# First-index one-hots made on GpSimd per token, and eight expert blocks beside the gate spreading in three rounded products

## The reference

```python
q = (hf @ wq).reshape(T, PEER_HEADS, 2, PEER_DQ // 2)
s = jnp.einsum('thcd,hckd->thck', q, subkeys).astype(jnp.float32)
v_top, i_top = lax.top_k(s, PEER_TOPK)
...
ids = jnp.take_along_axis(cand_i, best_pos, axis=-1)
g = jax.nn.softmax(best_s, axis=-1)
...
act = jax.nn.gelu(jnp.einsum('tkd,td->tk', ub, xb).astype(jnp.float32))
return jnp.einsum('tk,tkd->td', (gb * act).astype(xb.dtype), vb)
```

## Time and profile before

| | |
|---|---|
| time, median of 3 runs | 2134.61 us (2133.51 to 2137.69) |
| profiled execution, its own time | 2135.38 us |
| its span, first to last instruction | 2133.6 us |
| mean granted TensorE clock | 0.988 of full speed |
| spreading with blocks 12 to 19 | about 672.8 to 786.9 us of the span |
| expert blocks 20 and later | from 786.8 us |

### The profile page before, as it was taken

How to read it: one execution, slowest core, us unless ns; L and a number is a source line. 1 busy time by engine, 2 the same in 40 slices (tenths; PEclk the granted TensorE clock), 3 DMA queues, 4 the chain that set the end, 5 groups by cost and what they waited for, 6 DMA issues and landing times.

```text
span 2133.6 us, 31064 instructions
## 1 busy us (share of the span) xinstructions
PE 2069.0 (97%) x12256; PEld 1861.9 (87%) x12256; DVE 1383.8 (65%) x1840; ACT 742.7 (35%) x791; POOL 16.1 (1%) x30
## 2 busy tenths in 40 slices
PE   7999997999999998999999999999999999999997
PEld 5888886779988998999999999999999999999786
DVE  6675776747788986565555655555656555555697
ACT  2014112436312344334344343343443433433333
POOL 0000000000000000000000000000000000000000
PEclk8999999999999999999999999999999999999999
DMA  9999888645443657555565555554655556545894
GB/s 389 421 418 373 281 343 361 232 145 196 163 153 118 218 217 290 193 208 203 176 223 192 191 204 190 209 207 174 221 192 196 203 185 215 202 178 215 335 410 137
DMA packets 99209, 500.34 MB, mean 235 GB/s; under 512 B 8416, under 2 KB 41488, under 8 KB 42960
## 3 DMA queue, kind: packets, MB, share of 16 engines
q1 hardware_dynamic: 81840, 362.27, 46.0%
q10 hardware_dynamic: 13680, 112.20, 14.2%
q0 software_dynamic: 3632, 25.06, 3.0%
HBM read 477.32 MB, written 22.18 MB: 234 GB/s over the span
## 4 chain that ended last, share of the span: by engine, by line
PE 89%; DMA 7%; DVE 3%; issue 1%; ACT 1%; ACTq 0%; SPq 0%; DVEq 0%
PE ps L506 16%; PE ps L495 11%; PE ps L497 11%; PE ps L496 11%; PE ps L786 5%; PE ps L787 5%; PE ps L788 5%; PE ps L799 5%; PE ps L797 5%; PE ps L798 5%; DMA mod_first<-wmod 5%; PE ps L743 3%; PE ps L645 1%; PE ps L647 1%; PE ps L646 1%
## 5 line engine op out<-in xcount | busy, mean ns | idle before, releaser
L497 PE MATMUL ps<-h_hi,wlo 128*128 128x256 f32 x1952 | 553.6, 284 | 0.0
L495 PE MATMUL ps<-h_hi,whi 128*128 128x256 f32 x1728 | 490.3, 284 | 5.4 <-ACT act_u L1074 5.4
L496 PE MATMUL ps<-h_lo,whi 128*128 128x256 f32 x1728 | 490.2, 284 | 0.0
L1573 DVE TENSOR_TENSOR yacc<-yacc,ps 128x512 f32<-128x512 f32 x208 | 143.1, 688 | 368.0 <-PE ps L799 368.0
L497 PEld LDWEIGHTS ps<-h_hi,wlo 128*128 128x128 f32 x1952 | 375.7, 192 | 0.0
L1539 DVE TENSOR_TENSOR vlo<-vraw,vhi 128x2048 fp32r<-128x2048 f32 x116 | 260.7, 2288 | 137.9 <-ACT vhi L1120 137.9
L495 PEld LDWEIGHTS ps<-h_hi,whi 128*128 128x128 f32 x1728 | 332.9, 193 | 7.6 <-issue 5.6
L496 PEld LDWEIGHTS ps<-h_lo,whi 128*128 128x128 f32 x1728 | 332.9, 193 | 2.0
L1096 ACT ACTIVATE whi<-wraw 128x2048 fp32r<-128x2048 f32 x120 | 228.9, 1914 | 148.7 <-DMA wraw<-wst 146.1
L1535 DVE TENSOR_TENSOR wlo<-wraw,whi 128x2048 fp32r<-128x2048 f32 x120 | 269.4, 2284 | 16.6 <-ACT whi L1096 16.6
L1074 ACT ACTIVATE act_u<-ps 128x256 f32 (+1 forms) x128 | 49.0, 383 | 639.2 <-PE ps L497 576.3
(11 more groups left out here) (269 smaller groups left out, 2664.2 us busy)
## 6 DMA issues: line engine op xcount, KB each, us to landing
vraw<-vtab SPq DMA_DIRECT2D x116, 1024.0 KB, 6.8
wraw<-wst SPq DMA_DIRECT2D x111, 1024.0 KB, 4.8
wraw<-wst ACTq DMA_DIRECT2D x91, 1024.0 KB, 5.5
mod_ring<-wmod SPq DMA_DIRECT2D x58, 1024.0 KB, 11.3
mod_first<-wmod SPq DMA_DIRECT2D x22, 1024.0 KB, 20.2
gates_dram<-gstage ACTq DMA_DIRECT2D x4, 4096.0 KB, 16.9
gring<-gates_dram SPq DMA_DIRECT2D x64, 256.0 KB, 5.1
g_ring<-wmod POOLq DMA_DIRECT2D x16, 1024.0 KB, 9.5
```

Of the source, the lines that this page charges most:

```text
L495: mm(dst, hi, src_hi, start=first, stop=False)
L496: mm(dst, hi, src_lo, start=False, stop=False)
L497: return mm(dst, lo, src_hi, start=False, stop=last)
```

## The change

GpSimd makes `hot_a`, token by token, with its own semaphore (`one_hots_a`); VectorE keeps `hot_b`. Blocks 12 to 19 are multiplied as three rounded products. Their high halves go into four new buffers `first_whi` (ScalarE, `first_hi`, two blocks ahead), their low halves over `wraw` (VectorE, `first_lo`), in VectorE's list between groups of eight turns. The 12 blocks before and all after stay as they were, save the counts of the semaphores.

```diff
+        first_whi = [at(f"first_whi{i}", kb, [KD, P], F32R) for i, kb in enumerate((149.5, 77.5, 157.5, 165.5))]
...
             def spread(r_, n, first=False):
                 pe.wait_ge(s_hot, n + 1)
+                pe.wait_ge(s_hota, n + 1)
...
-            def chunk_and_spreads(j, n, i, k):
-                def between(kk):
+            def split_and_spreads(j, n, i, k):
+                if k == N_U + FIRST:
+                    pe.wait_ge(s_h, KD)
+                pe.wait_ge(s_wlo, n - (N_U + FIRST - 1))
+                pe.wait_ge(s_wev, n - 1)
+                hi = first_whi[(k - N_U - FIRST) % W_RING]
+                for kk in range(KD):
+                    r = three(ps_w[k % 2], hi[:, kk, :], wlo[:, j, kk, :], h_hi[:, kk, :], h_lo[:, kk, :],
+                              kk == 0, kk == KD - 1)
+                    if kk == KD - 1:
+                        r.then_inc(s_wmm, 1)
                     if (kk + 1) % (KD // per) == 0:
                         m = (k - N_U - FIRST) * per + kk // (KD // per)
                         spread(m % HOT_RING, i * (4 * per) + m, first=(m < HOT_RING and isinstance(n, int)))
-                chunk(j, n, i, k, src=h32, between=between)
...
+            def first_hi(b):
+                slot = (N_U + b) % W_RING
+                act.wait_ge(s_w[slot], turns(0, N_U + b, W_RING) * 16)
+                A(first_whi[(b - FIRST) % W_RING][:], wraw[:, slot], ACT.Copy).then_inc(s_whi, 1)
             for b in range(1, FIRST):
                 early_gelu(b)
+                if b == FIRST - 2:
+                    first_hi(FIRST)
...
+            first_hi(FIRST + 1)
             for tt in range(TT):
                 act.wait_ge(s_pkt, tt + 1)
                 A(picks[:, :, tt * P:(tt + 1) * P], ps_spread[tt][:, 0:3], ACT.Copy).then_inc(s_pkr, 1)
...
                     early_gelu(b)
+                    if b + 2 < EARLY:
+                        first_hi(b + 2)
...
-            dve.wait_ge(s_pkr, 2)
+            def first_lo(b):
+                slot = (N_U + b) % W_RING
+                dve.wait_ge(s_whi, b - FIRST + 1)
+                V.tensor_tensor(wlo[:, slot], wraw[:, slot], first_whi[(b - FIRST) % W_RING][:].bitcast(F32),
+                                ALU.subtract).then_inc(s_wlo, 1)
             def one_hots(r_, n, first=False):
                 if not first:
                     dve.wait_ge(s_gmm, n - (HOT_RING - 1))
-                V.tensor_tensor(hot_a[:, r_], iota.unsqueeze(1).to_broadcast([P, GT, P]),
-                                picks[:, 0, bass.ds(n * GT, GT)].unsqueeze(2).to_broadcast([P, GT, P]), ALU.is_equal)
                 for t in range(GT):
                     b, g = (picks[:, i, bass.ds(n * GT + t, 1)] for i in (1, 2))
                     r = V.tensor_scalar(hot_b[:, r_, t, :], iota, b, g, ALU.is_equal, ALU.mult)
                 r.then_inc(s_hot, 1)
+            first_lo(FIRST)
+            dve.wait_ge(s_pkr, 2)
             for n in range(HOT_RING):
                 one_hots(n, n, True)
-            with dve.Fori(1, SPREADS // HOT_RING) as i:
+            turns_each = SPREADS // HOT_RING // (EARLY - FIRST)
+            for b in range(FIRST + 1, EARLY):
+                first_lo(b)
+                with dve.Fori((b - FIRST - 1) * turns_each + 1, (b - FIRST) * turns_each + 1) as i:
+                    for r_ in range(HOT_RING):
+                        one_hots(r_, i * HOT_RING + r_)
+            with dve.Fori((EARLY - FIRST - 1) * turns_each + 1, SPREADS // HOT_RING) as i:
...
+            def one_hots_a(r_, n, first=False):
+                if not first:
+                    pool.wait_ge(s_gmm, n - (HOT_RING - 1))
+                for t in range(GT):
+                    r = nc.gpsimd.tensor_scalar(hot_a[:, r_, t, :], iota, picks[:, 0, bass.ds(n * GT + t, 1)], None,
+                                                ALU.is_equal)
+                r.then_inc(s_hota, 1)
+            pool.wait_ge(s_pkr, 2)
+            for n in range(SPREADS):
+                one_hots_a(n % HOT_RING, n, n < HOT_RING)
```

More of the change, by code:

```diff
@@ L347, in hybrid_block @@
                                           sem("picks_transposed"), sem("picks_read"))
-        s_hot, s_gmm, s_gev = sem("one_hots"), sem("gates_spread"), sem("gates_staged")
+        s_hot, s_hota, s_gmm, s_gev = sem("one_hots_b"), sem("one_hots_a"), sem("gates_spread"), sem("gates_staged")
         s_gst = [sem(f"gates_stored{q}") for q in range(TQ)]
@@ L751, in between @@
                         spread(m % HOT_RING, i * (4 * per) + m, first=(m < HOT_RING and isinstance(n, int)))
-                chunk(j, n, i, k, src=h32, between=between)
             for n in range(N_U + FIRST, N_U + FIRST + 4):
-                chunk_and_spreads(n % 4, n, 0, n)
-            stretch(pe, N_U + FIRST + 4, N_U + EARLY, chunk_and_spreads)
+                split_and_spreads(n % 4, n, 0, n)
+            stretch(pe, N_U + FIRST + 4, N_U + EARLY, split_and_spreads)
             def u_block(j, n, i, k):
-                if k == N_U + EARLY:
-                    pe.wait_ge(s_h, KD)
-                pe.wait_ge(s_wlo, n - (N_U + EARLY - 1))
+                pe.wait_ge(s_wlo, n - (N_U + FIRST - 1))
                 pe.wait_ge(s_wev, n - 1)
@@ L815, in tail_split @@
                     return (s_vlo, (N_TAIL + 2 * i + g) * GB), v_ring[g * GB:g * GB + GB]
-                return (s_wlo, 4 * i + (NB + g * GB - EARLY)), w_ring[g * GB:g * GB + GB]
+                return (s_wlo, 4 * i + (NB + g * GB - FIRST)), w_ring[g * GB:g * GB + GB]
             def tail_y0(n):
@@ L1533, in w_lo @@
             def w_lo(j, n):
-                dve.wait_ge(s_whi, n - (N_U + EARLY - 1))
+                dve.wait_ge(s_whi, n - (N_U + FIRST - 1))
                 V.tensor_tensor(wlo[:, j], wraw[:, j], whi[:, j].bitcast(F32), ALU.subtract).then_inc(s_wlo, 1)
```

## The result

The changed kernel takes 2189.59 us (median of 4 runs, 2187.35 to 2190.30) against 2135.24 us before (4 runs): ratio 1.0252, 95% interval 1.0234 to 1.0270. It is 54 us slower. The side was forecast and the time lies in the range, but I had given 23 us: the size was wrong by more than a factor of two.

A forecast was written before the change was run, and what follows sets the result against it. TensorE bounded the kernel before; GpSimd would become the bound at 1.57 + 0.55 = 2.12 us per turn. From 673.4 us, 64 turns end the stage 23.1 us late: 2158 us against 2134.6, range 2126 to 2200.

The forecast's parts named there:

- TensorE's part: Stage of blocks 12 to 19: rounded products 0.12 us apart cut TensorE's turn from 1.75 to 1.61 us, at most 9.0 us.
- VectorE's part: Stage: without hot_a, VectorE needs 1.02 + 0.285 = 1.31 us per turn, under TensorE's 1.61.
- GpSimd's part: Stage: four hot_a instructions per turn, guessed at 0.39 us each, 1.57 us per turn; called the unknown.
- My upper bound of 529 ns: GpSimd's hot_a instruction: bounded from above by its row for issuing a transfer, 2.12 us per turn.
- taken alone it would just fit: Stage: GpSimd's 1.57 us per turn, without interference, would just stay under TensorE's 1.61.
- the next term: Stage: 0.55 us per turn added to GpSimd's turn for VectorE's moving data in the same memory.
- What the engines do to each other: Stage: VectorE's data movement delays GpSimd, 4 x 0.065 for hot_b plus 0.285 for the low half, 0.55 us per turn.
- The second rival, full exclusion: Stage: GpSimd and VectorE never run together, 2.88 us per turn, 2206 us; chance 0.20 for beyond 2.5 us per turn.
- Where it begins: Stage start: block 13's rounding and block 12's low half come first; GpSimd starts at 673.4, first turn near 675.2 us.
- The rival of TensorE's clock: Stage: short waits lower TensorE's clock, turn about 3.2 us, over 90 us late; counted in the exclusion's chance of 0.20.
- The cover of the low half's wait: Once per block: VectorE's low half waits for ScalarE's rounding; 6.4 us in all, covered by TensorE's 7.2 us of ready work.

The follow-up runs named there:

- e8: e4 with block 12's low half made during the wait for the gates' exp and picks copied before block 13's rounding; 2131.98 us, 0.9983 of the kernel before.
- e4: The whole change, but GpSimd makes hot_a only for odd turns and VectorE for even ones; 2131.70 us, ratio 0.9985 to the kernel before.
- e3: The whole change, but GpSimd compares with a constant instead of the token's column of picks; 2171.37 us.
- e6: The whole change, but GpSimd makes a turn's hot_a in one 128 x 512 instruction comparing with a constant; 2137.42 us.
- e7: The whole change, but GpSimd makes a turn's hot_a in two 128 x 512 instructions, subtraction then comparison with zero; 2201.87 us, 1.0310 of the kernel before.
- e5: The whole change, but after the first four turns VectorE writes only one column of one token's hot_b per turn; 2186.41 us.

## Why the prediction came out as it did

**TensorE's part: right.** Rounded tiles start 0.12 us apart in the stage, and where others keep up a turn is 1.61 us (e8).

**VectorE's part: right in that it fits, a little too low.** It waited 51 us for TensorE in the stage. But beside GpSimd its `hot_b` start 0.29 us apart on average and not 0.255, so its turn is nearer 4 x 0.29 + 0.285 = 1.44 us than 1.31. That changes nothing here; in e4 it is what makes VectorE the bound.

**GpSimd's part: the step that failed.** I had 0.39 us per instruction, halfway between VectorE's 0.255 and GpSimd's transfer row of 529 ns; it is 0.577. 256 x 0.187 = 48 us were missing. Both rows were unfit: neither that of another engine's comparison nor that of issuing a transfer says anything of what a column costs GpSimd, which is 2.58 ns by e3 and e6 and makes up 0.33 of the 0.577 us. My upper bound of 529 ns was no bound at all, and "taken alone it would just fit" was false: alone it needs 2.31 us against TensorE's 1.61, or 1.75 before. The forecast missed by 31 us (54 against 23) and not by 48 only because the next term was about 20 us too large: that is luck. The estimate from the Trainium skill's "GPSIMD Engine Reference" (sections 3.1 and 4.1), one-input work at roughly line rate, 0.11 to 0.28 us, lies even further off: this comparison needs 2.58 ns per column, which at the 1.2 GHz of the Trainium skill's section is an estimate of 3.1 cycles. The 2.6 cycles that the Trainium skill gives there for two-input arithmetic, an estimate of 1.11 us for 512 columns, fit the 1.07 us of the subtraction in e7.

**What the engines do to each other: the kind half right, the size too large.** I had 0.55 us per turn, 35 us in all: 0.265 for `hot_b` and 0.285 for the low half. The first is next to nothing (e5: 0.5 us in all). The second is 1.8 to 2.1 us per low half, 15.5 us in all, against 18 by my price. Where I was wrong about `hot_b` is the direction: it is VectorE that loses, 0.29 instead of 0.255 us each in the change, where its waiting covers it, and 0.37 beside the long GpSimd instructions of e6.

The second rival, full exclusion, gave 2206 us, 16 above the result; it was near for the wrong reason, since it took the same too low price and a too large overlap. The rule of the Trainium skill behind it ("SBUF — State Buffer", Who interferes with whom) agrees for instructions with two inputs: GpSimd's instruction is held while the low half beside it runs (2.40 us each at 737 us), and in e7 VectorE's `hot_b` is held for the 1.07 us of GpSimd's subtraction. For VectorE's `tensor_scalar` beside GpSimd's `tensor_scalar`, both reading one tensor, the measurement differs: GpSimd keeps its 0.577 us, and VectorE loses only 0.03 us (the change) to 0.12 us (e6) per instruction on average, much less than the length of GpSimd's.

**Where it begins.** The low half of block 12 and the rounding of block 13 did come first, and GpSimd began 2.97 us after the exp's start, against 3.03 in my sum. The first turn is 5.83 us after the exp's start instead of 4.31, and not 4.8 as I had it, since it waits for GpSimd's first four instructions.

**The rival of TensorE's clock.** The granted clock of the execution fell only to 0.983 from 0.988, and in the stage to 0.91 (672 to 835 us), so for short stretches it was at the lower level. It cost nothing: GpSimd has no gap between its instructions, and in e5, at 1.00 from 690 us on, the stage is only 0.7 us shorter.

**The cover of the low half's wait** held: VectorE waited 9.7 us in all for the roundings, but GpSimd's account above fills the whole stage, and nothing is left for ScalarE.

The corrected sum is 64 x 2.31 + 8 x 1.89 + 0.4 = 163.4 us of GpSimd, where mine had 64 x 2.12 = 135.7. It accounts for the stage, which is 51.6 of the 54 us. For the remaining 2 to 3 us there is no cause shown.

## What to carry to other kernels

Price an engine that has no arithmetic in the trace by its cost per column and not by a row of another engine, and if no row gives it, carry a wide range: here one instruction cost 2.3 times VectorE's (0.577 against 0.255 us) and one column five times. Offloading helps only to the share at which the slower engine keeps step: GpSimd at 0.577 us per one-hot could take half of them at TensorE's 1.61 us per turn, all of them never. And a gain of 0.14 us on the bound engine needs that much slack on every engine that feeds it, lumps such as a 2.3 us low half included.

## What the runs showed of the hardware that I had not expected

- GpSimd's comparison with a scalar, float32, 128 partitions: 0.17 us fixed and 2.58 ns per column (0.498 us for 128 columns in e3, 1.49 for 512 in e6, starts apart); a scalar read from memory adds 0.08 us. Its two-input subtraction of 512 columns takes 1.07 us (e7), less than the comparison.
- A GpSimd instruction beside a two-input VectorE instruction is held up for most of that one's length: 2.38 to 2.70 us from start to start instead of 0.58 beside 2.3 us low halves; its row is 3.57 us instead of 1.49 there in e6, and 1.13 instead of 0.60 beside a 0.68 us `hot_a` in e4.
- Between GpSimd's one-input comparison and VectorE's two-at-a-time `tensor_scalar` it is VectorE that loses: 0.255 us each alone, 0.29 beside 0.58 us GpSimd instructions, 0.37 beside 1.49 us ones, while GpSimd's own pace stays at 0.577 us with and without them.
- Beside GpSimd's two-input subtraction the same `tensor_scalar` waits until that ends: 1.05 us instead of 0.34 (e7).
